# Expert biases of a mixture-of-experts block: loaded and split for all experts at once, and picked by a selector column

## The reference, cut to what matters

```python
logits = (h @ router_w) + router_b
top_logit, top_idx = lax.top_k(logits, TOP_K)          # 4 of 32
gates = jax.nn.softmax(top_logit, axis=-1)
...
gu = xb @ w_gate_up[e] + b_gate_up[e]                  # 1024 -> 2048
gate, up = jnp.split(gu, 2, axis=-1)
gate = jnp.minimum(gate, SWIGLU_LIMIT)
up = jnp.clip(up, -SWIGLU_LIMIT, SWIGLU_LIMIT)
act = (up + 1.0) * (gate * jax.nn.sigmoid(SWIGLU_ALPHA * gate))
y = act @ w_down[e] + b_down[e]                        # 1024 -> 1024
return y * g[:, None]
```

## Time and profile before

| | |
|---|---|
| median of 3 runs | 2544.07 us (2539.43 to 2545.36) |
| the profiled execution, its own time | 2538.18 us |
| its span (first to last instruction) | 2536.6 us |
| mean granted TensorE clock | 0.957 of full speed |
| PE busy / weight loads busy | 2293.7 / 1891.9 us |
| DVE busy / ACT busy / POOL busy | 1642.3 / 1276.9 / 322.7 us |
| the expert items | from about 658 us to about 2485 us |

### The profile page before, as it was taken

The page is one execution under the profiler, slowest core; times in us unless marked ns, Lnnn a source line. Parts: engine busy times, 40 slices in busy tenths (PEclk is TensorE's granted clock), DMA queues, the critical chain, the costliest instruction groups (busy, mean ns, idle before and its releaser), DMA issues.

```text
span 2536.6 us, 35696 instructions
## 1 busy us (share of the span) xinstructions
PE 2293.7 (90%) x11202; PEld 1891.9 (75%) x11203; DVE 1642.3 (65%) x1730; ACT 1276.9 (50%) x1424; POOL 322.7 (13%) x305
## 2 busy tenths in 40 slices
PE   6999778796699999999999999999999999999991
PEld 5889545695578877877777777778888777888771
DVE  4311357555476578698779888866656896656762
ACT  5111358433354466466557667644444665445452
POOL 0000000012111011022211212211110121111100
PEclk8999979997799999999999999999999999999996
DMA  5111200433577679599779999966666997666844
GB/s 194 35 50 50 83 1 1 150 84 109 195 257 245 186 274 319 193 367 337 262 251 347 331 349 335 354 229 212 202 194 203 356 335 270 201 201 212 272 132 149
DMA packets 266914, 540.85 MB, mean 213 GB/s; under 512 B 14802, under 2 KB 31468, under 8 KB 266868
## 3 DMA queue, kind: packets, MB, share of 16 engines
q1 hardware_dynamic: 248884, 487.94, 54.5%
q0 software_dynamic: 17984, 52.29, 8.6%
HBM read 501.07 MB, written 39.11 MB: 213 GB/s over the span
## 4 chain that ended last, share of the span: by engine, by line
PE 54%; DVE 17%; issue 10%; ACT 3%; DMA 1%; ACTq 1%; DVEq 0%; POOL 0%; SPq 0%; POOLq 0%
PE ps L642 50%; DVE w_lo L1463 3%; DVE last_slot L1463 2%; DVE hT_lo L1474 2%; DVE region_mem L1501 2%; DVE slots_between L1463 2%; PE ps L867 2%; ACT hT_hi L1096 2%; DVE work L1497 2%; DVE work L1490 1%; DVE work L1319 1%; PE ps L782 1%; DVE work L1506 1%; PE ps L860 1%; DVE mem_there L1468 1%
## 5 line engine op out<-in xcount | busy, mean ns | idle before, releaser
L642 PE MATMUL ps<-hT_hi,hT_lo 128*128 128x512 f32 (+1 forms) x4736 | 1513.6, 391 | 0.0
L642 PEld LDWEIGHTS ps<-hT_hi,hT_lo 128*128 128x128 f32 x4736 | 896.7, 190 | 184.5
L1096 ACT ACTIVATE hT_hi<-weight_ring 128x2048 fp32r<-128x2048 f32 x417 | 787.6, 1914 | 299.0 <-PE ps L642 256.7
L1463 DVE TENSOR_TENSOR slots_between<-weight_ring,hT_hi 128x2048 fp32r<-128x2048 f32 x245 | 554.7, 2289 | 150.2 <-ACT hT_hi L1096 145.3
L642 PE MATMUL ps<-slots_between,hT_lo 128*128 128x512 f32 x1344 | 524.6, 390 | 0.0
L642 PE MATMUL ps<-w_lo,hT_lo 128*128 128x512 f32 (+1 forms) x896 | 344.3, 384 | 0.0
L1463 DVE TENSOR_TENSOR w_lo<-weight_ring,hT_hi 128x2048 fp32r<-128x2048 f32 x140 | 319.7, 2284 | 31.2 <-ACT hT_hi L1096 31.2
L642 PEld LDWEIGHTS ps<-slots_between,hT_lo 128*128 128x128 f32 x1344 | 252.7, 188 | 53.4
L642 PEld LDWEIGHTS ps<-w_lo,hT_lo 128*128 128x128 f32 x896 | 173.9, 194 | 32.6
L1118 ACT ACTIVATE region_mem<-work 128x512 f32<-128x512 f32 x96 | 57.2, 621 | 272.8 <-DVE work L1490 272.8
L560 POOL DMA_INDIRECT residual_rows<-work,idx_now x48 | 94.0, 1959 | 485.8 <-ACT work L1135 411.2
(11 more groups left out here) (242 smaller groups left out, 2427.9 us busy)
## 6 DMA issues: line engine op xcount, KB each, us to landing
weight_ring<-in_w_gate_up SPq DMA_DIRECT2D x280, 1024.0 KB, 7.7
weight_ring<-in_w_down SPq DMA_DIRECT2D x140, 1024.0 KB, 5.1
weight_ring<-in_w_mix_in SPq DMA_DIRECT2D x10, 1024.0 KB, 8.5
weight_ring<-in_x SPq DMA_DIRECT2D x8, 512.0 KB, 8.3
weight_ring<-in_w_mix_out SPq DMA_DIRECT2D x4, 1024.0 KB, 5.0
work<-in_x SPq DMA_DIRECT2D x8, 512.0 KB, 5.5
residual_rows<-work SPq DMA_DIRECT2D x8, 512.0 KB
normed_rows<-work SPq DMA_DIRECT2D x8, 512.0 KB, 5.0
```

Source lines behind the costliest of these rows:

```text
L642: return pe.matmul(o, l, r, start=first, stop=last)
L1096: act.activation(w_high_part(u), ring[:, home(u), :], ACT.Copy).then_inc(s["w_high_made"], 1)
L1463: dve.tensor_tensor(w_low_part(u), ring[:, home(u), :], w_high_part(u).bitcast(f32), ALU.subtract)\
```

## The change

The gate-up biases of all 32 experts (32 rows of 2048) are loaded twice into partitions 0 to 63 of one region, the down biases (32 rows of 1024) twice into partitions 64 to 127, and the second copies once more elsewhere, as the source for the low parts: six transfers, once. ACT rounds both blocks in place, DVE writes the low parts over the second copies. A small constant `pick` has in partition p a one at column p mod 32. Per item ACT reads the item's expert number from the table and spreads that column of `pick` over 128 columns (`picked`). The bias matmul then takes 64 partitions of `picked` and of the bias region, from partition 0 for gate and up, from 64 for down. The loads, the ACT copies and the DVE subtractions of the biases in the loop are gone, and so are a memset on POOL and the waits on them.

```diff
-            def load_bias_gu(e):
-                for row in (0, 32):
-                    sp.dma_start(raw_gu[row:row + 4, :], b_gu[:, bass.ds(e, 1), :].rearrange("r e n -> r (e n)"))\
-                        .then_inc(s["bias_gu_in"], 16)
+            def load_biases():
+                for at, name in enumerate(("b_gate_up", "b_down")):
+                    sp.dma_start(bias_part(r_mem, at, 0), a[name][0]).then_inc(s["bias_in"], 16)
+                    sp.dma_start(bias_part(r_mem, at, 1), a[name][0]).then_inc(s["bias_in"], 16)
+                    sp.dma_start(bias_part(bias_again, at, 1), a[name][0]).then_inc(s["bias_in"], 16)
...
-            pool.memset(r_mem[:, 0:2 * HALF], 0.0).then_inc(s["bias_zero"], 1)
...
                     for b in range(nb):
                         pe.wait_ge(s_xlow[b], it + 1)
-                    pe.wait_ge(s["bias_gu_low"], it + 1)
-                if u == 8:
-                    pe.wait_ge(s["bias_d_low"], it + 1)
+                    pe.wait_ge(s["picked"], it + 1)
...
-                        pick_row = {"g": c, "u": 2 + c, "d": c}[side]
-                        mm(bank, pick[:, pick_row, :], pair_d if side == "d" else pair_gu, True, False)
+                        rows_of = slice(2 * EXPERTS, 4 * EXPERTS) if side == "d" else slice(0, 2 * EXPERTS)
+                        at = (D if side == "u" else 0) + HALF * c
+                        mm(bank, picked[rows_of, :], mem_r[rows_of, at:at + HALF],
+                           True, False)
...
                 high_unit(it, 3)
-                bias_d_high(it)
...
                 with act.If(size_next > 0):
-                    bias_gu_high(it + 1)
                     high_unit(it + 1, 0)
+                    expert = act.value_load(table[0:1, bass.ds(it + 2, 1)], min_val=0, max_val=EXPERTS - 1)
+                    act.wait_ge(s["w_used"], it * 12 + (HI_SLOTS + 10))
+                    act.activation(picked[:, :], pick[:, bass.ds(expert, 1)].bitcast(f32).broadcast_to((P, P)), ACT.Copy)\
+                        .then_inc(s["picked"], 1)
...
-            bias_gu_high(0)
+            act.wait_ge(s["bias_in"], 16 * 6)
+            for at in range(2):
+                act.activation(bias_part(mem_r, at, 0, 2), bias_part(r_mem, at, 0, 2), ACT.Copy).then_inc(s["bias_high"], 1)
...
                 low_unit(it, 3)
-                bias_low(it, pair_d, raw_d, s["bias_d_high"], s["bias_d_low"])
                 gates(it, 0, nb)
...
                 with dve.If(size_next > 0):
-                    bias_low(it + 1, pair_gu, raw_gu, s["bias_gu_high"], s["bias_gu_low"])
                     low_unit(it + 1, 0)
```

More of the change, by code:

```diff
@@ L174, in hymba_kernel, with bias_part @@
         up_b = work[:, 5120:6144].rearrange("p (b n) -> p b n", b=BLOCKS)
[L175 to L178, removed]
+        bias_at = ((0, 2 * D), (2 * EXPERTS, D))
         sig_b = r_mem[:, 2048:3072].rearrange("p (b n) -> p b n", b=BLOCKS)
+        bias_again = r_bias[:, D:3 * D]
+        def bias_part(region, at, part, n=1):
+            row, cols = bias_at[at]
+            return region[row + part * EXPERTS:row + (part + n) * EXPERTS, 0:cols]
         def w_high_part(u):
@@ L209, in hymba_kernel @@
         router_b = sb("router_b", [P, EXPERTS])
-        pick = ctx.enter_context(nc.sbuf_tensor("pick", [P, 4, P], f32r))
+        pick = ctx.enter_context(nc.sbuf_tensor("pick", [P, EXPERTS], f32r))
+        picked = ctx.enter_context(nc.sbuf_tensor("picked", [P, P], f32r))
         line = wk[0:HEADS, 5, :]
@@ L459, in _ @@
             sp.wait_ge(s["e_oT"], NT)
-            sp.wait_ge(s["bias_zero"], 1)
-            load_bias_gu(0)
-            load_bias_d(0)
+            load_biases()
             for u in range(SLOTS):
@@ L473, in _ @@
                     e = sp.value_load(table[0:1, bass.ds(k + 2, 1)], min_val=0, max_val=EXPERTS - 1)
-                    sp.wait_ge(s["bias_gu_low"], k + 1)
-                    load_bias_gu(e)
                     for u in range(SLOTS):
@@ L940, in _ @@
             pe.wait_ge(s["pick_made"], 1)
+            pe.wait_ge(s["bias_low"], 2)
             pe.sem_inc(s["w_used"], HI_SLOTS)
@@ L1096, in high_unit @@
                 act.activation(w_high_part(u), ring[:, home(u), :], ACT.Copy).then_inc(s["w_high_made"], 1)
[L1098 to L1105, removed]
             def x_high(b, it):
@@ L1172, in _ @@
                 act.activation(w_high_part(u), ring[:, home(u), :], ACT.Copy).then_inc(s["w_high_made"], 1)
-            bias_gu_high(0)
+            act.wait_ge(s["bias_in"], 16 * 6)
+            for at in range(2):
+                act.activation(bias_part(mem_r, at, 0, 2), bias_part(r_mem, at, 0, 2), ACT.Copy).then_inc(s["bias_high"], 1)
+            act.wait_ge(s["pick_made"], 1)
+            act.activation(picked[:, :], pick[:, 0:1].bitcast(f32).broadcast_to((P, P)), ACT.Copy).then_inc(s["picked"], 1)
             for b in range(BLOCKS):
@@ L1363, in _ @@
             dve.wait_ge(s["consts_made"], 1)
-            dve.tensor_tensor(pick[:, :, :], ident[:, 0:4].unsqueeze(2).broadcast_to((P, 4, P)),
-                              ident[:, 32:36].unsqueeze(2).broadcast_to((P, 4, P)), ALU.add).then_inc(s["pick_made"], 1)
+            for row in (0, 2 * EXPERTS):
+                some = slice(row, row + 2 * EXPERTS)
+                ins = dve.tensor_tensor(pick[some, :], ident[some, row:row + EXPERTS], ident[some, row + EXPERTS:row + 2 * EXPERTS],
+                                        ALU.add)
+            ins.then_inc(s["pick_made"], 1)
             for i in range(NT + 2):
@@ L1464, in low_unit @@
                     .then_inc(s["w_low_made"], 1)
-            def bias_low(it, pair, raw, high, low):
-                dve.wait_ge(high, it + 1)
-                dve.tensor_tensor(pair[32:64, :], raw[32:64, :], pair[32:64, :].bitcast(f32), ALU.subtract).then_inc(low, 1)
             def x_low(b, it):
@@ L1545, in _ @@
                 low_unit(0, u)
-            bias_low(0, pair_gu, raw_gu, s["bias_gu_high"], s["bias_gu_low"])
+            for at in range(2):
+                dve.wait_ge(s["bias_high"], at + 1)
+                dve.tensor_tensor(bias_part(mem_r, at, 1), bias_part(bias_again, at, 1), bias_part(mem_r, at, 1).bitcast(f32),
+                                  ALU.subtract).then_inc(s["bias_low"], 1)
             for b in range(BLOCKS):
```

13 lines of the change are left out of this document (2 added, 11 removed).

## The result

The changed kernel takes **2585.39 us** in the median of four runs (2585.36 to 2587.64). The kernel before, measured beside it, takes 2543.06 (2539.43 to 2545.36). The ratio is 1.0174 with a 95% interval of 1.0161 to 1.0187: the change makes the kernel 1.7% slower. The profiled execution took 2585.36 us, its span is 2583.8.

The account below looks back on a forecast made before the run. PE was taken to bound two-block items, a chain through DVE one-block items. 2538.2 + 56.6 + 19.1 - 22.5 + 1 = 2592, plus 3 for the median: 2595 us; own range 2575 to 2610, over the cases 2553 to 2622.

Parts of the forecast that it names:

- The change of form empties PE: On PE, switching between 128 and 64 partitions around each bias matmul stops weights loading ahead: 0.41 us per bias matmul.
- three gaps: Matmul starts around the bias matmul on PE: 0.32, 0.43 and 0.34 us apart, together 1.09 in place of 0.68.
- Two-block items: Items of two blocks, bound by PE: twelve bias matmuls less 0.57 us of waiting, 4.35 us each, 56.6 over 13.
- One-block items: Items of one block: unit 7 ends 2.05 us later, its product starts 0.91 later; 39.97 us each, 19.1 over 21.
- The clock: One-block items: PE's wait shrinks to about 1.1 us, so the 14 slowdowns to 1.2 GHz vanish, gaining 22.5 us.
- the rival in which they all stay: One-block items: clock falls remain with the full drain, since emptied moments count as idleness too; 2617 us, chance 0.17.
- ACT's selector, the initial split, the queues: ACT's per-item table read and copy, longer splits before the first item, work removed from ACT, SP, POOL: zero.
- The late-selector rival: On ACT, table read and copy exceed 0.81 us, delaying unit 2 and `results`: 15 us on 2523, 2538; chance 0.05.
- The sum: The whole kernel's terms added to the profiled execution of 2538.2 us: 2592 us.
- The 3 us added for the spread of the runs: Old median 5.9 us above its profiled execution, read as clock falls, most going: 3 us added, giving 2595.

Follow-up runs that it names:

- e1: The changed kernel with its bias matmul over all 128 partitions, zeros in the other weight's half of the selector rows: 2516.27 us, ratio 0.9895.
- e2: The kernel before, with only the bias matmul taking rows 0 to 63 in place of all 128: 2586.35 us, ratio 1.0165.
- e4: The kernel before, with only the bias matmul taking rows 0 to 95 in place of all 128: 2544.43 us, ratio 1.0003.
- e3: The changed kernel, with two-block items' bias matmuls in six pairs side by side in place of twelve single ones: 2560.72 us, ratio 1.0065.
- e5: e1 plus eight unread matmuls in one-block items, behind unit 8 and ahead of the wait for `turn_a`: 2501.70 us, ratio 0.9830.
- e6: e1 plus four unread matmuls in one-block items, behind unit 8 and ahead of the wait for `turn_a`: 2500.51 us, ratio 0.9826.
- e7: The changed kernel plus one unread DVE operation right ahead of `x_low(0)` in one-block items: 2604.75 us, ratio 1.0238.
- e9: The kernel before plus four unread matmuls behind unit 8 in one-block items: 2516.92 us, ratio 0.9893.
- e8: e1 plus four unread selector spreads on ACT ahead of the real one: 2517.04 us, ratio 0.9886.

## Why the prediction was right

It gave 2595 us, range 2553 to 2622, slower. Point by point:

- **The change of form empties PE.** Right, and shown by e1, e2 and e4. Rows 7 of another stage, 64-row matmuls that the attention happens to have, were enough to see it. The price was forecast at 0.41 us, put together from three gaps; the same three gaps are 0.32, 0.43 and 0.33 here, 0.40 more than 0.68. Around a bias matmul of full rows they take 0.70 (e1), not 0.68, so the price is 0.38, and averaged over an item it is (3.98 + 0.57) / 12 = 0.38 too. The Trainium skill, "TensorEngine Tiling", Key Properties, says that a change of the tiling mode drains TensorE. The trace agrees, with 0.38 to 0.40 us for going in and out. The pair of e3 shows that the change counts, not the matmul.
- **Two-block items.** Forecast 72.59 + 4.35 = 76.94 us, measured 76.56: 13 x 0.38 = 4.9 us too much, for the 0.03 us in the price.
- **One-block items.** Forecast 39.97, measured 39.78. The mechanism holds in each step. Unit 7 is done 1.90 us later (forecast 2.05); DVE used to take up the product 1.20 us later than PE allowed (forecast 1.14); so the product starts 0.70 us later (forecast 0.91), now waits for PE, 0.23 us, and the 0.71 us that DVE saves are lost. The term was mis-sized by 0.19 x 21 = 4 us, most of it five times the 0.03 us. PE's wait ahead of `turn_a` was forecast at 1.1 and is 1.33, since PE's own work grows by (39.78 - 1.33) - (39.06 - 2.65) = 2.04 us an item and not by 6 x 0.41 = 2.46. Beside six times the 0.03, the wait of 0.48 us ahead of unit 8, which is gone, had cost more than its length: from the end of unit 7 to that of unit 8 it is 4.64 us in the kernel before and 3.91 in e1, 0.25 more than the wait.
- **The clock.** Forecast no falls, measured 1 in 21; the rival in which they all stay would have had 14. Right in size, and e5, e6, e7 and e9 show that the wait ahead of `turn_a` makes them. That rival's reason, that emptied moments count as idleness too, is not refuted: 8 falls with the 64-row form at 1.66 us against none with full rows at 1.68 speak for it. The forecast was right because 1.33 us were short enough, not because the form is harmless, and there is some luck in it: at the same 1.33 us the profiled executions of e3 and e2 had 4 and 5 falls.
- **ACT's selector, the initial split, the queues.** Forecast at nothing, and they cost nothing: e1 gains the 0.71 us an item in full, and e8 has room for four more spreads. The late-selector rival took 0.81 us as the point from which an item grows; that was too strict. (The six transfers of the biases are 1.18 MB, not 1.15.)
- **The start.** The first bias matmul comes 1.2 us later than before (659.03 against 657.78 us), behind PE's wait for DVE's split of the first gathered rows, which lasts 2.7 us in both. The forecast had nothing there; the cause is not traced.
- **From the sum to the median.** The sum gave 2592, the execution took 2585.4; the two items' sizes account for 8.9 of the difference, and the one fall gives back 1.6. The 3 us added for the spread of the runs were wrong to add: the changed kernel hardly falls, so three of its four runs lie within 0.05 us of each other. The reading of the old spread behind it fits e9 but is not shown: without falls the old kernel has 2516.92, 26 us less, which would be 16 falls in a median run where the profiled one had 14; yet the four runs of e9 still lie 3.5 us apart, with no fall in the slowest, so falls are not all of the spread.

What the change meant to do is worth 1.05% by itself (e1); the form of one matmul in 25 (6 of 150 a block) took that and 1.7% more. Part of the 1.05% is fewer falls (10 in place of 14 in the profiled executions).

## What to carry to other kernels

A matmul that contracts over 64 rows among full ones is not cheaper here but 0.4 us dearer, for the way in and out of its form; pad its operands with zeros to the rows of its neighbours, or put such matmuls side by side (two were tried here). Before you count on time freed on an engine, look who waits for whom a step later: DVE's 0.71 us were worth 0.73 an item while PE waited for DVE and nothing once DVE waited for PE. And a wait of the tensor engine can cost time beyond its own length, 1.6 us for each fall of the clock here: measure the clock behind each wait, and try unread work in it, or shift the wait.

## What the runs showed of the hardware

- A bias matmul of 64 rows between 128-row ones costs 0.38 to 0.40 us, two side by side 0.40 to 0.41; one of 96 rows costs nothing that can be measured (2544.43 against 2543.96 us).
- One fall of the clock costs 1.6 us. How many there are, by PE's wait ahead of the turn: with full rows none in 21 at 0.3, 1.2, 1.5 and 1.7 us, 10 in 21 at 2.15 (in two kernels), 14 and 17 in 21 at 2.14 with another wait of 0.5 us that ends 5.4 us ahead of the turn (the kernel before and e4); that other wait with 1.2 us ahead of the turn gives none (e9). With the 64-row form 1, 5 and 4 in 21 at 1.33 us (the change, e2, e3), 8 in 21 at 1.66. I had expected a gradual rise with the wait; with full rows there is no fall up to 1.7 us. These are counts of one execution each. What the chip counts beside the wait stays open.
- The kernels without a fall in the profiled execution span 1.2 to 3.5 us over their runs (e6_warm_4 1.2, e9_before_warm_4 3.5), the kernel before 2.8 to 5.9 in its lots: they may repeat somewhat better, but the two overlap.
